# A modulation ring of four places in x's memory instead of two places of its own, for the first projection of a two-block transformer kernel

## The chip, the cores and the metric

One core of one Trainium2 chip runs the whole kernel in one launch. The metric is the device time of that core in microseconds, as the median of several executions. The engines that matter here are TensorE (PE; PEld is its weight load), VectorE (DVE), ScalarE (ACT), GpSimd (POOL) and SyncE (SP), whose queue issues most of the DMA transfers in the order in which they stand there.

## What is computed

Two transformer blocks on one sequence of 256 tokens of width 2048, in float32. The first block mixes by HGRN2 and gated delta heads, the second by four kinds of attention. Both take six modulation vectors from a small input c. Cut to what matters:

```python
def first_block(x, c, w_ada, b_ada, ..., w_in, ...):
    mod = silu(c) @ w_ada + b_ada                       # 2048 x 12288
    sh_m, sc_m, gt_m, sh_f, sc_f, gt_f = split(mod, 6)
    h = rmsnorm(x, pre_mix_norm) * (1.0 + sc_m) + sh_m
    proj = h @ w_in                                     # 2048 x 8208
    o_hg  = hgrn2_group(proj[..., :HG_COLS], ...)
    o_gdn = gdn_group(proj[..., HG_COLS:], ...)
    y = concat(o_hg, o_gdn) @ w_out
    x = x + gt_m * rmsnorm(y, post_mix_norm)
    ...
def reference(...):
    return second_block(first_block(x, ...), c_2, ada_w_2, ..., w_in_2, ...)
```

The parts of `mod` after the first two (sh_m, sc_m) are needed only after the mixing, so their columns of `w_ada` are loaded and summed in the background of other phases.

## The kernel before, in words

x is kept transposed in SBUF as `core.xT` (16 KB a partition). The first projection (`phase_in_1`, line 1594) computes h @ w_in in float32 accuracy from three products of rounded parts: each weight tile is split by ScalarE into a high part (L1983) and by VectorE into a low part (L2142, the weight less its high part), and TensorE makes high x high (L1826), high x low (L1833) and low x high (L1835). A piece of this work is a **slot**: a weight tile of 128 x 512. Four slots are a **group**, and one refill of 1 MB in two halves of 512 KB brings its weights; eight groups (32 slots) are a **turn**; there are eight turns. The parts lie in four places (`w`, KG = 4), so ScalarE may be at most four slots ahead of TensorE. Between the slots a `Pace` runs the head work of HGRN2 and the convolutions: programs that go on at slots written out by hand. In slots 34 and on, TensorE also multiplies the 16 gate columns (`gates()`, L1713), whose weights ScalarE's queue loads after slot 22 (L1991).

**SP's queue.** The weights lie in a ring of two groups, so refill g can only be issued when the subtraction in group g - 2 is done (`refill`, L104: the first half waits for that group's third slot, the second for its fourth). For turn i, refill q is thus issued at about slot 4q - 5 of the turn. Behind some refills stand loads of w_ada for the modulation (`ada.load_when_free`, L241), 512 KB each, eight a turn in turns 2 to 7. They go round a ring, and load q waits until VectorE has done the steps that used that place before:

```python
        steps = KT * self.per_turn
        queue.wait_ge(self.core.ada_steps, i * steps + (KT * self.chunks0 + AK * (q - self.slots + 1)))
```

While such a wait lasts, everything behind it in SP's queue stands. Which load stands behind which refill is written out in `AFTER_REFILL` (L1581; numbers from 8 on are loads 0 and 1 of the next turn), and `BEHIND_PAIR` (L1582) for turn 1. VectorE's 16 steps of a turn (L284, L288, two for each load) run in slots 2 + 3n/2 of the turn, that is 2, 3, 5, 6, 8, 9, ... 20, 21, 23, 24, each after the subtraction of its slot. Load 3 is thus used in slots 11 and 12, load 6 in 20 and 21, load 7 (steps 14 and 15) in 23 and 24. The ring has two places and lies in the eight tiles `GG` of `core.big`, where the last turn's output goes at the end.

In slots 28 to 59 VectorE makes 32 steps for two other chunks (`pair_ada`). Their loads are issued by POOL's queue (L238; the first four as soon as the parts of h are made, just ahead of slot 27). VectorE's queue is in order: if the first pair load is not there, the subtraction of slot 29 stands behind the step that waits for it.

**What follows.** `phase_gdn` (L2166) makes the gated delta heads; its loads of w_ada go by POOL and SP has no program in it. x is read again in the entry to the first feed-forward part. In the second block's mixer (`phase_mixer`, L2813) x is stored to device memory (`core.x_kept`, L3213), its place is used for weight parts, and it is loaded back at the end (L2886). The mixer has a modulation ring of its own with `MOD_RING` = 4 places of 256 KB (L3258, steps at L3355 and L3359, 16 steps in 48 slots).

Of the kernel before, what the change touches and what calls it, by code (L numbers as in the profile page):

```python
# [29 lines left out]
HH = 8  # L30
# [130 lines left out]
AK = 2  # L161
ASLOTS = 4
FIRST_ASLOTS = 10
IN_1_ASLOTS = 2
# [31 lines left out]
class Ada:  # L196
# [4 lines left out]
    def __init__(self, ctx, nc, core, parts, turns, slots=ASLOTS, ring=None, acc=None, folded=True, rows=None):  # L201
        self.slots, self.landed, self.folded = slots, core.ada_landed[slots], folded
# [5 lines left out]
        self.landed0, self.chunks0 = core.ada_landed_n[slots], core.ada_chunks  # L208
        core.ada_landed_n[slots] += turns * self.per_slot
# [1371 lines left out]
AFTER_REFILL = {2: (2, 3), 3: (4,), 4: (5,), 5: (6, 7), 6: (8,), 7: (9,)}  # L1581
# [9 lines left out]
ADA_SUM_SLOT, GATE_SLOT, GATE_LOAD_SLOT = 28, 34, 22  # L1591


def phase_in_1(nc, core, t, w_ada, w_in):
# [32 lines left out]
    with ExitStack() as ctx:  # L1627
        s = {n: ctx.enter_context(nc.semaphore(n)) for n in steps}
        for_heads = Ring(ctx, nc, "hgrn_bank", (4, 5, 6))
        ring = flat(GG, HH).rearrange("p (s k n) -> p s k n", s=IN_1_ASLOTS, k=AK)  # L1630
# [16 lines left out]
                  rows=ada_rows[:, 2:])  # L1647
# [28 lines left out]
        @block.sync  # L1676
        def _(sp):
            setup_sync(sp)
            for g in range(2 * QUARTERS - 2, st.groups):
                i, q = g // st.unit, g % st.unit  # L1680
                refill(sp, core, st, i, q)
                for n in (BEHIND_PAIR if i == 1 else AFTER_REFILL).get(q, ()):
                    if 2 <= i + n // st.unit < st.turns:
                        ada.load_when_free(sp, i - 2 + n // st.unit, n % st.unit)
            prefetch(sp, core, core.streams["out_1"])
# [20 lines left out]
        def _(pe):  # L1706
            def gates():
                yield from pace.until(GATE_SLOT)
                pe.wait_ge(core.gates_in_x_moved, 16)
# [136 lines left out]
        def _(act):  # L1846
# [129 lines left out]
            for slot in range(SLOTS):  # L1976
# [12 lines left out]
                if slot == GATE_LOAD_SLOT:  # L1989
                    with nc.allow_non_contiguous_dma("the 16 gate columns"):  # L1990
                        act.dma_start(core.w_gates[:], w_in[0, :, 8192:8208].rearrange("(k p) n -> p k n", p=P)  # L1991
                                      ).then_inc(core.gates_in_x_moved, 16)
                if i and slot % TILES in (0, 2):
# [172 lines left out]
def phase_gdn(nc, core, w_ada):  # L2166
# [22 lines left out]
    with ExitStack() as ctx:  # L2189
# [35 lines left out]
        made = {}  # L2225

# [582 lines left out]
MOD_CHUNK, MOD_CHUNKS, MOD_SLOT, MOD_SLOTS, MOD_RING = 16, 2, 56, 56, 4  # L2809
# [3 lines left out]
def phase_mixer(nc, core, entry, mix, t, w_ada_2):  # L2813
# [28 lines left out]
    with ExitStack() as ctx:  # L2842
# [22 lines left out]
        mod_ring = spare[:, 0:8, :].rearrange("p a b -> p (a b)").rearrange("p (s n) -> p s n", s=MOD_RING)  # L2865
# [15 lines left out]
        def _(sp):  # L2881
# [5 lines left out]
            sp.wait_ge(core.gates_in_x_moved, 48)  # L2887
# [183 lines left out]
        def _(act):  # L3071
# [120 lines left out]
            def high(c, kg):  # L3192
                g, width = st.first + 4 * c + kg, IN_2[c][1]
                for k in range(KG):
# [9 lines left out]
                    elif k % 2 == 0:  # L3204
                        if MIX_DEEP_SLOT + KG <= slot < MIX_DEEP_SLOT + 2 * KG:
                            act.wait_ge(core.gates_in_x_moved, 32)
# [340 lines left out]
def build(nc, t, out):  # L3547
    with ExitStack() as ctx:
# [33 lines left out]
        core.ada_landed = {n: [sem(f"ada_landed_{n}_{s}") for s in range(n)] for n in (IN_1_ASLOTS, ASLOTS, FIRST_ASLOTS)}  # L3582
        core.ada_landed_n = {IN_1_ASLOTS: 0, ASLOTS: 0, FIRST_ASLOTS: 0}
# [121 lines left out]
```

## Time and profile before

| what | us |
|---|---|
| median of 3 runs | 2793.84 |
| lowest and highest | 2792.79, 2795.73 |
| the execution that was profiled, timed | 2793.61 |
| its span in the profile | 2791.9 |
| first projection, slots 0 to 255 | about 47 to 548 |
| gated delta phase | 554 to about 640 |
| mixer of the second block | about 1525 to 1900 |

In a row of a timeline stand the start in us, the time in us from the first to the end of the last instruction merged into it, engine, line, operation, out<-in and the count; in square brackets the idle time of the engine before it and what ended it. "SPq" is SP's queue issuing transfers. In a row of waits stand the sum of us, how many times, and the longest. A row of a stretch has the busy us of each engine with its count of instructions, TensorE's granted clock (PEclk, share of 2.4 GHz), the mean busy share of the 16 DMA engines, and GB/s.

### The profile page before, as it was taken

The numbers are of one execution on the slowest core, as the hardware profiler recorded it, in microseconds if no ns is written. First come the engines' busy times: TensorE is split into PE (matmuls) and PEld (weight loads), VectorE is DVE, ScalarE is ACT, GpSimd is POOL, SyncE is SP. The second block draws the span as 40 slices with busy tenths as digits, with TensorE's granted clock in tenths as the row PEclk, the third lists the DMA queues.
The fourth block names the chain that finished last, engine by engine and source line by source line (L and its number), as shares of the span: only waits on it lengthen the run. The fifth ranks groups of instructions, "written<-read, shape, count | busy, mean of one in ns | idle before, by whom it ended". The sixth has DMA issues, their size and how long they took to land. (4 is left out here: it accounts for less than half of the span.)

```text
span 2791.9 us, 49277 instructions
## 1 busy us (share of the span) xinstructions
PE 2666.6 (96%) x18997; PEld 2382.1 (85%) x18997; DVE 1950.2 (70%) x2726; ACT 1393.1 (50%) x2232; POOL 305.7 (11%) x447
## 2 busy tenths in 40 slices
PE   7899999988999999999999999998999999999998
PEld 4579998887878888999998898887878888889998
DVE  2288987677777777898998566656787655555564
ACT  3355757645455555445444454555344444444454
POOL 1011413031011111121211010001011000000000
PEclk9999999999999999999999999999999999999999
DMA  9777676536488878898994765537578655655564
GB/s 364 296 261 234 227 238 195 194 114 228 158 282 275 277 270 277 309 335 307 319 336 141 207 205 159 149 114 247 191 272 293 218 181 181 193 186 186 177 195 133
DMA packets 290452, 636.57 MB, mean 228 GB/s; under 512 B 30754, under 2 KB 51686, under 8 KB 289766
## 3 DMA queue, kind: packets, MB, share of 16 engines
q1 hardware_dynamic: 239264, 486.88, 52.8%
q0 software_dynamic: 39424, 142.62, 14.7%
q10 hardware_dynamic: 11590, 4.64, 0.7%
q8 instruction: 122, 2.00, 0.3%
q14 instruction: 52, 0.43, 0.0%
HBM read 629.87 MB, written 4.19 MB: 227 GB/s over the span
## 5 line engine op out<-in xcount | busy, mean ns | idle before, releaser
L1229 DVE TENSOR_TENSOR weight_parts<-weights,weight_parts 128x1024 fp32r<-128x1024 f32 x584 | 707.2, 1221 | 267.3 <-ACT weight_parts L1149 265.9
L1149 ACT ACTIVATE weight_parts<-weights 128x1024 fp32r<-128x1024 f32 x584 | 607.4, 1057 | 572.4 <-PE accumulators L1340 225.7
L1329 PE MATMUL accumulators<-h_parts,weight_parts 128*128 128x512 f32 x2816 | 776.8, 397 | 20.7 <-DVE h_parts L1216 8.5
L1329 PEld LDWEIGHTS accumulators<-h_parts,weight_parts 128*128 128x128 f32 x2816 | 484.1, 190 | 91.7 <-DVE h_parts L872 10.1
L1340 PEld LDWEIGHTS accumulators<-h_parts,weight_parts 128*128 128x128 f32 x2944 | 451.4, 190 | 73.3 <-DVE weight_parts L1229 13.0
L1340 PE MATMUL accumulators<-h_parts,weight_parts 128*128 128x256 f32 x2944 | 472.5, 282 | 9.0 <-DVE weight_parts L1229 8.9
L1833 PE MATMUL accumulators<-in_h_parts,in_weight_parts 128*128 128x256 f32 x1024 | 263.6, 289 | 20.7 <-DVE in_weight_parts L2142 20.4
L2142 DVE TENSOR_TENSOR in_weight_parts<-weights,in_weight_parts 128x512 fp32r<-128x512 f32 x256 | 186.2, 745 | 113.6 <-ACT in_weight_parts L1983 113.0
L1835 PE MATMUL accumulators<-in_h_parts,in_weight_parts 128*128 128x256 f32 x1024 | 260.0, 286 | 0.0
L1373 PE MATMUL accumulators<-h_parts,weight_parts 128*128 128x512 f32 x864 | 236.5, 395 | 2.8 <-issue 1.8
L1983 ACT ACTIVATE in_weight_parts<-weights 128x512 fp32r<-128x512 f32 x256 | 154.9, 627 | 147.6 <-PE accumulators L1835 103.9
L1833 PEld LDWEIGHTS accumulators<-in_h_parts,in_weight_parts 128*128 128x128 f32 x1024 | 199.0, 194 | 26.4 <-DVE in_weight_parts L2142 25.8
L1393 PE MATMUL accumulators<-h_parts,weight_parts 128*128 128x256 f32 x864 | 216.8, 283 | 0.1
L1395 PE MATMUL accumulators<-h_parts,weight_parts 128*128 128x256 f32 x864 | 216.6, 283 | 0.0
L1835 PEld LDWEIGHTS accumulators<-in_h_parts,in_weight_parts 128*128 128x128 f32 x1024 | 199.1, 194 | 0.0
L1826 PE MATMUL accumulators<-in_h_parts,in_weight_parts 128*128 128x256 f32 x1024 | 179.2, 298 | 15.1 <-DVE in_h_parts L1661 9.6
L1826 PEld LDWEIGHTS accumulators<-in_h_parts,in_weight_parts 128*128 128x128 f32 x1024 | 144.2, 195 | 44.9 <-issue 23.9
L1373 PEld LDWEIGHTS accumulators<-h_parts,weight_parts 128*128 128x128 f32 x864 | 147.7, 189 | 23.3 <-issue 2.1
L1393 PEld LDWEIGHTS accumulators<-h_parts,weight_parts 128*128 128x128 f32 x864 | 165.9, 192 | 0.5 <-DVE weight_parts L1229 0.5
L1395 PEld LDWEIGHTS accumulators<-h_parts,weight_parts 128*128 128x128 f32 x864 | 165.9, 192 | 0.0
L288 DVE SCALAR_TENSOR_TENSOR ada_sums<-h_t,c_act,ada_sums 128x512 f32<-128x512 f32 x224 | 159.8, 746 | 4.6 <-DMA h_t<-in_ada_w 4.4
L238 POOL DMA_DIRECT2D h_t<-in_ada_w x112 | 80.3, 718 | 720.9 <-DVE ada_sums L288 238.7
(426 smaller groups left out, 3702.2 us busy)
## 6 DMA issues: line engine op xcount, KB each, us to landing
weights<-in_w_ff SPq DMA_DIRECT2D x256, 512.0 KB, 5.8
weights<-in_w_in SPq DMA_DIRECT2D x160, 512.0 KB, 5.3
wide<-in_w_ada SPq DMA_DIRECT2D x112, 512.0 KB, 10.0
h_t<-in_ada_w POOLq DMA_DIRECT2D x112, 512.0 KB, 6.7
weights<-in_ffn_w_gate SPq DMA_DIRECT2D x88, 512.0 KB, 4.6
weights<-in_ffn_w_up SPq DMA_DIRECT2D x88, 512.0 KB, 4.5
weights<-in_ffn_w_down SPq DMA_DIRECT2D x88, 512.0 KB, 4.2
weights<-in_w_out SPq DMA_DIRECT2D x64, 512.0 KB, 5.6
```

The source lines that it names most:

```text
L288: ins = nc.vector.scalar_tensor_tensor(out=acc, in0=w, scalar=number, in1=acc, op0=ALU.mult, op1=ALU.add)
L1149: nc.scalar.activation(w[:, held:held + take, 0, :], core.ring[:, q % RING, k:k + take, :], ACT.Copy).then_inc(core.high_ready, take)
L1229: ins = nc.vector.tensor_tensor(w[:, held:held + take, 1, :], core.ring[:, q % RING, k:k + take, :], w[:, held:held + take, 0, :].bitcast( ...
L1329: nc.tensor.matmul(both(nt), high, x[:, kt].rearrange("p a t -> p (a t)"), start=(kt == 0), stop=False, skip_group_check=True)
L1340: ins = nc.tensor.matmul(rest(nt) if two else acc(c, nt), w[:, held, 1, nt * P:(nt + 1) * P], x[:, kt, 0, :], start=False, stop=(kt == KT ...
L1373: nc.tensor.matmul(both(nt), w[:, held, 0, cols[nt]], xk.rearrange("p a t -> p (a t)"), start=first, stop=False, skip_group_check=True)
L1393: nc.tensor.matmul(accs[nt], w[:, held, 0, cols[nt]], xk[:, 1, :], start=False, stop=False, skip_group_check=True)
L1395: ins = nc.tensor.matmul(accs[nt], w[:, held, 1, cols[nt]], xk[:, 0, :], start=False, stop=(last and nt % 2 == 1), skip_group_check=True)
L1826: nc.tensor.matmul(acc(c, nt), w[:, k, 0, nt * P:(nt + 1) * P], x[:, kt, 0, :], start=(kt == 0 and nt % 2 == 0), stop=False, skip_group_ch ...
L1833: nc.tensor.matmul(acc(c, nt), w[:, k, 0, nt * P:(nt + 1) * P], x[:, kt, 1, :], start=False, stop=False, skip_group_check=True)
L1835: ins = nc.tensor.matmul(acc(c, nt), w[:, k, 1, nt * P:(nt + 1) * P], x[:, kt, 0, :], start=False, stop=(kt == KT - 1 and nt % 2 == 1), sk ...
L2142: ins = nc.vector.tensor_tensor(w[:, k, 1, :], core.ring[:, g % RING, part, :], w[:, k, 0, :].bitcast(F32), ALU.subtract)
```

## The change

The first projection's modulation ring gets four places and moves into the memory of x. To make room, x is stored to device memory by ScalarE's queue after slot 26 (2 MB) and loaded back by SP's queue at the start of the gated delta phase. SP waits for the store before the first load into the new ring (behind refill 15), and the gates' products wait for a count of 32 on the same semaphore, so for the store as well. The table of loads becomes one load behind each refill from 1 to 6 and two behind refill 7: load 7, before behind refill 5, now stands behind refill 6, and loads 2 and 3 behind refills 1 and 2. The ring gets semaphores of its own, and the mixer's ring shrinks from four places to two. The counts that later waits name go up by 32.

```diff
-IN_1_ASLOTS = 2
+IN_1_ASLOTS = 4
...
+    def __init__(self, ctx, nc, core, parts, turns, slots=ASLOTS, ring=None, acc=None, folded=True, rows=None, landed=None):
+        landed = landed or slots
+        self.slots, self.landed, self.folded = slots, core.ada_landed[landed], folded
...
-AFTER_REFILL = {2: (2, 3), 3: (4,), 4: (5,), 5: (6, 7), 6: (8,), 7: (9,)}
+AFTER_REFILL = {1: (2,), 2: (3,), 3: (4,), 4: (5,), 5: (6,), 6: (7,), 7: (8, 9)}
 BEHIND_PAIR = {7: (8, 9)}
...
+X_KEPT_SLOT = 26
...
-        ring = flat(GG, HH).rearrange("p (s k n) -> p s k n", s=IN_1_ASLOTS, k=AK)
+        ring = core.xT[:].rearrange("p a b -> p (a b)").rearrange("p (s k n) -> p s k n", s=IN_1_ASLOTS, k=AK)
...
                 refill(sp, core, st, i, q)
+                if g == 2 * st.unit - 1:
+                    sp.wait_ge(core.gates_in_x_moved, 32)
                 for n in (BEHIND_PAIR if i == 1 else AFTER_REFILL).get(q, ()):
...
             def gates():
                 yield from pace.until(GATE_SLOT)
-                pe.wait_ge(core.gates_in_x_moved, 16)
+                pe.wait_ge(core.gates_in_x_moved, 32)
...
+                if slot == X_KEPT_SLOT:
+                    act.dma_start(core.x_kept, core.xT[:].rearrange("p a b -> p (a b)")
+                                  ).then_inc(core.gates_in_x_moved, 16)
...
+        @block.sync
+        def _(sp):
+            sp.dma_start(core.xT[:].rearrange("p a b -> p (a b)"), core.x_kept).then_inc(core.gates_in_x_moved, 16)
+            sp.wait_ge(core.gates_in_x_moved, 48)
...
-MOD_CHUNK, MOD_CHUNKS, MOD_SLOT, MOD_SLOTS, MOD_RING = 16, 2, 56, 56, 4
+MOD_CHUNK, MOD_CHUNKS, MOD_SLOT, MOD_SLOTS, MOD_RING = 16, 2, 56, 56, 2
...
-        mod_ring = spare[:, 0:8, :].rearrange("p a b -> p (a b)").rearrange("p (s n) -> p s n", s=MOD_RING)
+        mod_ring = spare[:, 0:2 * MOD_RING, :].rearrange("p a b -> p (a b)").rearrange("p (s n) -> p s n", s=MOD_RING)
...
-            sp.wait_ge(core.gates_in_x_moved, 48)
+            sp.wait_ge(core.gates_in_x_moved, 80)
...
-                            act.wait_ge(core.gates_in_x_moved, 32)
+                            act.wait_ge(core.gates_in_x_moved, 64)
```

## Rows read from the trace of the kernel before

**Rows 1.** Head of the page.
```profile
span 2791.9 us, 49277 instructions
```

**Rows 2.** Busy times of stretches of the first projection.
```profile
150.00:200.00 50.00, 50.00 (x351) 40.51 (x350) 41.33 (x75) 24.18 (x33) 6.59 (x9) 1.00 0.72 251
...
318.00:378.00 60.00, 53.26 (x519) 51.23 (x518) 55.52 (x71) 42.42 (x82) 24.55 (x24) 1.00 0.65 217
...
435.00:500.00 65.00, 65.00 (x508) 58.97 (x507) 40.72 (x56) 45.84 (x90) 12.59 (x16) 1.00 0.62 198
```

**Rows 3.** Waits from 200 to 552 us: sum, times, longest.
```profile
ACT in_weight_parts L1983 <- DMA weights<-in_w_in: 27.3, 16, 4.1
...
PE accumulators L1833 <- DVE in_weight_parts L2142: 18.9, 17, 2.1
...
DVE turn_sums L288 <- DMA wide<-in_w_ada: 1.3, 2, 1.1
```

**Rows 4.** VectorE in order of time, in turns 4, 5 and 7.
```profile
352.37 2.27 DVE L2142 TENSOR_TENSOR in_weight_parts<-weights,in_weight_parts 128x512 fp32r<-128x512 f32 x2
...
358.07 0.74 DVE L288 SCALAR_TENSOR_TENSOR turn_sums<-wide,c_act,turn_sums 128x512 f32<-128x512 f32 x1
...
361.05 0.69 DVE L2142 TENSOR_TENSOR in_weight_parts<-weights,in_weight_parts 128x512 fp32r<-128x512 f32 x1 [1.33 <-ACT in_weight_parts L1983]
...
406.18 1.28 DVE L2142 TENSOR_TENSOR in_weight_parts<-weights,in_weight_parts 128x512 fp32r<-128x512 f32 x2
...
412.59 0.74 DVE L288 SCALAR_TENSOR_TENSOR turn_sums<-wide,c_act,turn_sums 128x512 f32<-128x512 f32 x1
...
530.77 1.29 DVE L2142 TENSOR_TENSOR in_weight_parts<-weights,in_weight_parts 128x512 fp32r<-128x512 f32 x2
...
535.40 0.74 DVE L288 SCALAR_TENSOR_TENSOR turn_sums<-wide,c_act,turn_sums 128x512 f32<-128x512 f32 x1
538.49 0.69 DVE L2142 TENSOR_TENSOR in_weight_parts<-weights,in_weight_parts 128x512 fp32r<-128x512 f32 x1 [2.35 <-ACT in_weight_parts L1983]
```

**Rows 5.** SP's queue in turn 3: loads 2 and 3.
```profile
265.32 7.15 SPq L238 DMA_DIRECT2D wide<-in_w_ada  x2
```

**Rows 6.** SP's queue at the end of turn 1: loads 0 and 1.
```profile
195.78 4.17 SPq L238 DMA_DIRECT2D wide<-in_w_ada  x2
```

**Rows 7.** Landing of loads at L238: at 214.6 us, at 502.3 us, all 46 after 210.
```profile
DMA to landing us min/median/max: 7.0/7.0/7.0
...
DMA to landing us min/median/max: 6.2/6.2/6.2
...
DMA to landing us min/median/max: 3.6/4.7/7.0
```

**Rows 8.** Busy times of stretches around the end of turn 0.
```profile
125.00:130.00 5.00, 3.97 (x32) 3.90 (x33) 3.38 (x5) 1.73 (x4) 3.03 (x4) 1.00 0.07 9
...
135.00:140.00 5.00, 2.94 (x13) 2.94 (x14) 0.69 (x1) 1.83 (x4) 0.00 (x0) 0.51 1.03 413
140.00:145.00 5.00, 3.54 (x16) 3.25 (x16) 3.39 (x7) 2.34 (x7) 0.72 (x1) 0.50 0.94 317
```

**Rows 9.** VectorE's first pair step and TensorE's product that waits behind it.
```profile
141.17 0.49 DVE L284 TENSOR_SCALAR turn_sums<-wide,c_act 128x512 f32<-128x512 f32 x1 [3.43 <-DMA wide<-in_w_ada]
...
142.31 0.58 PE L1833 MATMUL accumulators<-in_h_parts,in_weight_parts 128*128 128x256 f32 x1 [1.46 <-DVE in_weight_parts L2142]
```

**Rows 10.** The mixer: landing of x_kept's store, of the refill behind, of five before.
```profile
DMA to landing us min/median/max: 9.0/9.0/9.0
...
DMA to landing us min/median/max: 8.7/8.7/8.7
...
DMA to landing us min/median/max: 3.1/3.2/4.5
```

**Rows 11.** A stretch early in the gated delta phase.
```profile
560.00:565.00 5.00, 5.00 (x24) 2.96 (x23) 2.65 (x6) 3.11 (x5) 4.30 (x11) 1.00 0.45 177
```

**Rows 12.** VectorE in the mixer behind the ring's first three steps.
```profile
1619.72 1.09 DVE L3468 TENSOR_TENSOR in_weight_parts<-weights,in_weight_parts 128x896 fp32r<-128x896 f32 x1 [3.04 <-ACT in_weight_parts L3210]
```

More of the change, by code:

```diff
@@ L196 @@
 class Ada:
-    def __init__(self, ctx, nc, core, parts, turns, slots=ASLOTS, ring=None, acc=None, folded=True, rows=None):
-        self.slots, self.landed, self.folded = slots, core.ada_landed[slots], folded
+    def __init__(self, ctx, nc, core, parts, turns, slots=ASLOTS, ring=None, acc=None, folded=True, rows=None, landed=None):
+        landed = landed or slots
+        self.slots, self.landed, self.folded = slots, core.ada_landed[landed], folded
         self.nc, self.core, self.turns = nc, core, turns
@@ L207, in __init__ @@
         self.per_slot = self.per_turn * AGROUPS // slots
-        self.landed0, self.chunks0 = core.ada_landed_n[slots], core.ada_chunks
-        core.ada_landed_n[slots] += turns * self.per_slot
+        self.landed0, self.chunks0 = core.ada_landed_n[landed], core.ada_chunks
+        core.ada_landed_n[landed] += turns * self.per_slot
         core.ada_chunks += turns * self.per_turn
@@ L1646, in phase_in_1 @@
         ada = Ada(ctx, nc, core, [(w_ada, 0, 2 * NT + 2, 1)], LAST - 1, IN_1_ASLOTS, ring, pair_ada.acc,
-                  rows=ada_rows[:, 2:])
+                  rows=ada_rows[:, 2:], landed="in_1")
         taps = big[:, HG:HG + 6, :].rearrange("p (a b) t -> p a b t", a=2)
@@ L3581, in build @@
         core.scaled, core.factored = sem("input_normalized"), sem("input_factored")
-        core.ada_landed = {n: [sem(f"ada_landed_{n}_{s}") for s in range(n)] for n in (IN_1_ASLOTS, ASLOTS, FIRST_ASLOTS)}
-        core.ada_landed_n = {IN_1_ASLOTS: 0, ASLOTS: 0, FIRST_ASLOTS: 0}
+        core.ada_landed = {name: [sem(f"ada_landed_{name}_{s}") for s in range(n)] for name, n in (
+            ("in_1", IN_1_ASLOTS), (ASLOTS, ASLOTS), (FIRST_ASLOTS, FIRST_ASLOTS))}
+        core.ada_landed_n = {"in_1": 0, ASLOTS: 0, FIRST_ASLOTS: 0}
         core.ada_steps, core.ada_sums_ready, core.ada_sums_taken = (
```

## Prediction

> **What bounds the kernel now.** I read four views in this order. First the page's head: the span is 2791.9 us, and the same execution was timed at 2793.61 us [rows 1]. The sum below is made against that 2793.61; the median of the three runs is 2793.84, 0.2 us away, so the one stands for the other. Then the busy times by stretch inside the first projection, where the ring that changes is used [rows 2]. From 435 to 500 us TensorE is busy for 65.00 of 65 us. From 318 to 378 it is idle for 6.7 us while VectorE is busy for 55.5 of 60. So a turn is bound by TensorE where its extra products are many and by VectorE where the head work is, while the DMA engines are at about two thirds. Third, the waits from 200 to 552 us [rows 3]: ScalarE waits 27.3 us for refills in 16 places, which is what the change can remove. But TensorE's idle time, 18.9 us, is put down to VectorE's subtraction of the low parts, not to a load. What earlier refills can give back is therefore not 27.3 us, only the part of the 18.9 us for which VectorE itself was short of work. Fourth, VectorE in order of time [rows 4]: it stood idle for a refill's high part for 1.33 us before 361.05 and for 2.35 us before 538.49. I found no third such place ahead of a gap of TensorE, so the gain in sight is at most 3.7 us.
>
> **Part 1, SP's queue.** Today load 3 stands in SP's queue ahead of refill 3, and its wait (for VectorE's step at slot 6) ends only as that refill's place comes free. The two loads hold SP from 265.32 to 272.47, and the refill goes out behind them [rows 5]. Load 7 does the same ahead of refill 6. With four places these waits are satisfied long before, so the first halves of the two refills leave about 1 us earlier (one step of VectorE and the issue) in each of six turns. The same holds at the hand-over to turn 2, where the pair's last steps keep SP until 199.95 before refill 16 [rows 6]: that refill comes some 3 us earlier, but ScalarE then waits for TensorE's last tile of the turn anyway. I count nothing for it, and up to 1 us in the range.
>
> **Part 2, load 7.** The new list puts load 7 straight behind refill 6. Refill 6's second half waits for VectorE's subtraction in slot 19 of the turn; load 7 is used by step 14, in slot 23, after that slot's subtraction. Today load 7 leaves at slot 18, alone. What does a load take that leaves straight behind a refill? Load 2 does so today in each of six turns, and lands 6.2 to 7.0 us after its own issue (the last and the first of the six), which is 0.4 us behind the second half's [rows 7]. I take 6.6 + 0.4 = 7.0 us. Turn 4: slot 19's subtraction ends at 353.5 (the first of the two at 352.37), so the load lands at 360.5; step 14 is due at 358.07, and from there to the idle stretch before 361.05 there are 1.65 us of work, so slot 24's subtraction comes at 362.15, not 361.05: 1.1 us later. Turn 5: 406.8 + 7.0 = 413.8 against step 14 at 412.59: 1.2 us. Turn 7: 531.4 + 7.0 = 538.4, and 0.74 us of work, is 539.1 against 538.49: 0.7 us [rows 4]. All three lie just ahead of a place where TensorE waits for VectorE, so I pass them on whole. In turns 2 and 3 I reckon with half a microsecond where TensorE has slack, in turn 6 with none. Sum: 3.0 us. Note that the two idle stretches which could be won, in turns 4 and 7, are the very ones in which load 7 is late now: the refill is no longer late, the load behind it is. Bounds: 0 (the quickest of 46 loads lands in 3.6 us [rows 7]) and 5. Loads 2 to 6 have five slots or more to land, loads 8 and 9 ten: 0. SP's new wait before loads 8 and 9 of turn 1 is for a store issued four refill groups and more earlier: 0.
>
> **Part 3, x goes out.** ScalarE's queue issues a store of 2 MB after slot 26; the issue itself costs nothing, since ScalarE then idles for refill 7. But the store meets the worst place of the phase. The gate columns' load has kept the DMA engines at 9 GB/s; once it is through, all that has queued (two refills, the pair's four first loads) moves at 413 and 317 GB/s with the engines full [rows 8]. 2.10 MB more at 413 GB/s is 5.1 us. And a delay here finds no slack: VectorE waits 3.43 us for the first pair load, until 141.17; its next subtraction is what TensorE waits 1.46 us for, at 142.31 [rows 9]; from 150 to 200 us TensorE is busy for 50.00 of 50 [rows 2]. The nearest row for what such a store does to its neighbours is in the mixer: the same store takes 9.0 us, and a refill issued 2 us behind it takes 8.7 where five before it took 3.2 in the median, so it is held for 5.5 us [rows 10]. Bounds: 0 (the pair load, issued just before the store, goes wholly ahead) and 5.5. I take 4.5, near the upper end, because a part of that load is through before the store starts. Refill 8, behind the store, lands up to 5 us later too; ScalarE may run four slots ahead of TensorE, which is itself 4.5 us later by then: covered. The gates' products now wait for the store at slot 34, five slots after the stall, by when it has landed: 0, at most 1. TensorE's granted clock is 0.51 and 0.50 from 135 to 145, the lower of its two levels (1.2 GHz), after it idled [rows 8, 9]; a longer idle moves that stretch along and may lengthen it by 0 to 3 us; I take 0.
>
> **Part 4, x comes back.** 2 MB on SP's queue at the start of the delta phase, beside the loads there. From 560 to 565 us the DMA engines are at 0.45 [rows 11], SP has nothing else to do in that phase, and x is first read after it. What hides the load is that idle DMA time; without it it would cost about 5 us. I take 0, in the range 0 to 1.
>
> **Part 5, the mixer.** Its modulation ring has two places instead of four, so a load leaves only when the step before the previous one has ended. Steps are three slots apart by the code, and loads of twice the size land in 4.7 us in the median [rows 7]. Only the third load, whose steps come bunched at the start, would be late, by up to 3 us, and VectorE idles 3.04 us right behind it, before 1619.72 [rows 12]. 0, at most 1.
>
> **Sum.** 3.0 + 4.5 = 7.5 us: 2793.6 + 7.5 = 2801.1 us. The own range of this case is 2798 to 2806.
>
> **Rivals.** A measurement of this kernel can tell about 0.2% (5.6 us) from no change.
> (A, the forecast) The store and the late load 7 both cost: 2801.1. Chance 0.50, nine tenths of it past 5.6 us.
> (B) The store shares the DMA engines evenly instead of going first. The pair load then has a third of the engines where it had a half for its last 2 to 3 us, which costs 1 to 2.5 us: 1.8 + 3.0, so 2798.4. Against it speaks the refill of [rows 10], held for 5.5 of the store's 9.0 us; even sharing would have cost it about half. Chance 0.20, nearly all of it within 5.6 us.
> The Trainium skill states a rule for B ("DMA: Bandwidth & Descriptors", section "Issuing engines are not separate DMA queues"): transfers that different engines start run on the same DMA engines and interleave there. By that rule the total would be 2798.4, by the mixer's row 2801.1; rule and row differ, and I go by the row.
> (C, faster) The refills were what mattered: refills 3 and 6 leave 1 us earlier and no load is in flight beside them, so ScalarE is four slots ahead at every piece of head work, and the backlog of VectorE to which TensorE's 18.9 us are put down does not form. For it: 27.3 us of waiting for refills in 16 places [rows 3]. Against it: VectorE's 55.5 busy us of 60 where TensorE idles most [rows 2]. It decides if more than half of the 18.9 us goes and the store costs under 2: 2793.6 - 10 + 2 = 2785.6. Chance 0.18, of which 0.16 past 5.6 us.
> (D) The change does nothing that can be seen: the pair load is ahead of the store, and load 7 lands in 4 us. 2793 to 2795. Chance 0.12.
>
> **Range and chances.** 2790 to 2806.5 leaves out most of C and a small tail of A (a longer stretch at the low clock). Faster 0.16; within 5.6 us 0.36 (D, nearly all of B, the edges of A and C); slower 0.48.
>
> **What would show it.** The store: VectorE's wait for the first pair load grows from 3.4 to about 8 us, and TensorE's product that now starts at 142.3 starts near 147; if it stays where it is, part 3 is wrong. Load 7: VectorE's waits for the loads of w_ada come to over 3 us against 1.3 now [rows 3]; if they don't grow, part 2 is wrong. ScalarE's 27.3 us of waiting for refills should fall below 15 in any case but D; if TensorE's 18.9 us fall with them to under 10, C was right. The mixer and the delta phase should last as long as before within 1 us.

## The result, and the profile after

The changed kernel takes 2805.7 us (median of 19 runs) against 2792.8 us for the kernel before (19 runs beside them). The ratio is 1.0043, with a 95% interval of 1.0035 to 1.0052: 12 us slower, 10 to 14.5 by the interval. The forecast was 2801.1, slower, in a range of 2790 to 2806.5. The execution that was profiled took 2801.95 us, so the terms read from its profile add up to 8 us, not 12. One of the 19 runs took 3209.97 us and is not part of the ratio.

The head of the profile's page after; the span grew by 8.0 us [rows 1]:

```profile
span 2799.9 us, 49281 instructions
```

**The stop at the end of turn 0.** VectorE's first step for the pair, TensorE's product behind it, and two stretches (columns as in [rows 8]):

```profile
145.65 0.49 DVE L285 TENSOR_SCALAR turn_sums<-wide,c_act 128x512 f32<-128x512 f32 x1 [8.29 <-DMA wide<-in_w_ada]
```

```profile
146.79 0.58 PE L1837 MATMUL accumulators<-in_h_parts,in_weight_parts 128*128 128x256 f32 x1 [6.10 <-DVE in_weight_parts L2149]
```

```profile
140.00:145.00 5.00, 0.69 (x4) 0.49 (x3) 0.00 (x0) 0.57 (x2) 0.00 (x0) 0.84 1.00 415
145.00:150.00 5.00, 3.21 (x15) 3.21 (x16) 4.09 (x8) 2.39 (x6) 0.72 (x1) 0.50 0.86 301
```

The wait for the first pair load went from 3.43 to 8.29 us, TensorE's from 1.46 to 6.10 [rows 9]. From 140 to 145 the DMA engines are full while hardly any other engine works. TensorE starts again at the lower of its two clock levels, as before [rows 8], only five microseconds later.

**Who was issued first.** ScalarE and its queue (ACTq), POOL's queue, and the landing of the store (L1998):

```profile
123.17 1.06 ACT L1658 ACTIVATE in_h_parts<-h_t 128x1024 fp32r<-128x1024 f32 x1
123.39 0.38 ACTq L1998 DMA_DIRECT2D x_kept<-x_t  x1
124.13 2.18 ACT L1987 ACTIVATE in_weight_parts<-weights 128x512 fp32r<-128x512 f32 x4
```

```profile
124.89 3.04 POOL L239 DMA_DIRECT2D wide<-in_w_ada  x4 [110.64 <-ACT in_h_parts L1658]
```

```profile
DMA to landing us min/median/max: 22.0/22.0/22.0
```

The store leaves at 123.39, 1.5 us ahead of the four pair loads. They wait for the end of ScalarE's last high part of h (the 123.17 row, at 124.2). In ScalarE's program the store stands behind that instruction and behind the high parts of slots 24, 25 and 26, the first three of the 124.13 row, and yet it was issued before any of these three began: the issue didn't wait for the instructions ahead of it to run. I had the order the other way round. The store landed at 145.4, together with the first pair load (145.65).

**Load 7 and the other loads of w_ada.** Waits from 200 to 570 us (sum, times, longest), the landing of SP's 46 loads of w_ada, and VectorE where it waited for one: for load 7 in turn 4 (365.71), for load 6 and then load 7 in turn 5 (414.63 and 420.29), for load 7 in turn 7 (546.27):

```profile
PE accumulators L1837 <- DVE in_weight_parts L2149: 22.6, 22, 3.3
...
DVE turn_sums L289 <- DMA x_t<-in_w_ada: 8.6, 5, 3.4
ACT in_weight_parts L1987 <- DMA weights<-in_w_in: 7.9, 7, 2.6
```

```profile
DMA to landing us min/median/max: 5.2/6.7/9.2
```

```profile
365.71 1.22 DVE L289 SCALAR_TENSOR_TENSOR turn_sums<-x_t,c_act,turn_sums 128x512 f32<-128x512 f32 x1 [2.90 <-DMA x_t<-in_w_ada]
...
414.63 0.75 DVE L289 SCALAR_TENSOR_TENSOR turn_sums<-x_t,c_act,turn_sums 128x512 f32<-128x512 f32 x1 [0.98 <-DMA x_t<-in_w_ada]
...
420.29 0.75 DVE L289 SCALAR_TENSOR_TENSOR turn_sums<-x_t,c_act,turn_sums 128x512 f32<-128x512 f32 x1 [0.79 <-DMA x_t<-in_w_ada]
...
546.27 0.75 DVE L289 SCALAR_TENSOR_TENSOR turn_sums<-x_t,c_act,turn_sums 128x512 f32<-128x512 f32 x1 [3.42 <-DMA x_t<-in_w_ada]
```

Read against [rows 3]: ScalarE's waits for refills fell from 27.3 to 7.9 us, just what the ring was for. TensorE's waits for VectorE rose from 18.9 to 22.6 all the same, because VectorE now waits 8.6 us for loads of w_ada against 1.3. A load that leaves behind a refill lands in 6.7 us in the median; before, it was 4.7 [rows 7].

**Stages.** Start of a slot's first product, and the end of slot 255's four products high x high, in us, from the timelines of one profiled execution each (e1 to e10 are the experiments below; the slot's other eight products take 1.0 us more in each, so the first projection of the kernel before ends at 553, not at 548 as the table ahead of the prediction has it):

| | before | after | e1 | e2 | e3 | e9 | e10 |
|---|---|---|---|---|---|---|---|
| slot 28 | 137.1 | 136.7 | 137.1 | 136.5 | 136.5 | 137.1 | 137.2 |
| slot 32 | 147.6 | 152.4 | 147.7 | 152.1 | 145.6 | 153.0 | 153.0 |
| slot 64 | 209.2 | 214.1 | 209.3 | 213.7 | 207.3 | 214.7 | 214.6 |
| slot 255 | 552.1 | 560.5 | 559.1 | 554.1 | 548.7 | 558.1 | 564.3 |
| slot 64 to there | 342.9 | 346.4 | 349.8 | 340.4 | 341.4 | 343.4 | 349.7 |
| output projection starts | 642.9 | 651.7 | 647.4 | 643.8 | 639.3 | 649.5 | 656.4 |
| mixer's first product | 1523.7 | 1532.8 | 1531.2 | 1521.3 | 1520.6 | 1533.2 | 1540.5 |
| span | 2791.9 | 2799.9 | 2798.3 | 2788.9 | 2787.0 | 2801.4 | 2808.0 |
| runs, median | 2792.8 | 2805.7 | 2799.8 | 2798.0 | 2789.4 | 2801.0 | 2804.3 |

So after has +4.8 by slot 32 and +3.5 between slot 64 and the end of the phase; from there to the output projection +0.4; nothing more behind it.

The same stretch by turns, from the start of a turn to the start of the next (turn 7: to the start of slot 255), in us. e4 and e9 have the old ring and the old table of loads:

| turn | before | e4 | e9 | after | e10 | e1 | e2 | e3 |
|---|---|---|---|---|---|---|---|---|
| 2 | 52.5 | 52.5 | 52.5 | 53.1 | 53.3 | 53.3 | 52.5 | 52.5 |
| 3 | 56.6 | 56.6 | 56.8 | 55.7 | 55.8 | 55.7 | 55.7 | 55.7 |
| 4 | 59.4 | 60.2 | 59.8 | 61.0 | 61.0 | 60.4 | 58.8 | 59.8 |
| 5 | 57.1 | 57.2 | 57.2 | 58.6 | 59.4 | 58.8 | 58.3 | 58.3 |
| 6 | 64.8 | 64.8 | 64.8 | 64.8 | 64.8 | 64.8 | 64.8 | 64.8 |
| 7 | 51.8 | 53.6 | 51.7 | 52.6 | 54.7 | 56.1 | 49.6 | 49.6 |

After, e10 and e1 have load 7 behind refill 6; e2 and e3 have it behind refill 5.

**x back, and the mixer.** A stretch of the delta phase in which x comes back (its load is issued at 562.5), and VectorE behind the third load of the mixer's ring:

```profile
565.00:570.00 5.00, 5.00 (x29) 3.50 (x29) 2.39 (x10) 1.97 (x5) 4.55 (x10) 1.00 0.94 396
```

```profile
1623.61 0.75 DVE L3371 SCALAR_TENSOR_TENSOR wide<-wide,c_act 128x512 f32<-128x512 f32 x1
1627.47 1.09 DVE L3480 TENSOR_TENSOR in_weight_parts<-weights,in_weight_parts 128x896 fp32r<-128x896 f32 x1 [3.11 <-ACT in_weight_parts L3222]
```

TensorE is busy for 5.00 of 5 us while the DMA engines are at 0.94. In the mixer the third step (1623.61) shows no wait, and the idle time behind it is what it was (3.11 against 3.04 [rows 12]).

### The profile page after: what moved, and what is told of

It is laid out like the page before. It is cut to its first block and busy times, and to the rows that moved or that the text cites. A ratio compares the mean times of both kernels' runs of the same rounds, so it can differ in the third digit from the quotient of the medians.

```text
span 2799.9 us, 49281 instructions
## 1 busy us (share of the span) xinstructions
PE 2670.5 (95%) x18997; PEld 2385.2 (85%) x18997; DVE 1949.3 (70%) x2726; ACT 1393.2 (50%) x2232; POOL 302.8 (11%) x447
## 3 DMA queue, kind: packets, MB, share of 16 engines
q1 hardware_dynamic: 239408, 488.98, 53.1%
## 5 line engine op out<-in xcount | busy, mean ns | idle before, releaser
L1330 PE MATMUL accumulators<-h_parts,weight_parts 128*128 128x512 f32 x2816 | 778.8, 398 | 18.9 <-DVE h_parts L1217 8.5
L1374 PEld LDWEIGHTS accumulators<-h_parts,weight_parts 128*128 128x128 f32 x864 | 147.7, 189 | 24.0 <-DVE weight_parts L1230 2.1
```

The lines of the kernel that those rows point to most:

```text
L1330: nc.tensor.matmul(both(nt), high, x[:, kt].rearrange("p a t -> p (a t)"), start=(kt == 0), stop=False, skip_group_check=True)
L1374: nc.tensor.matmul(both(nt), w[:, held, 0, cols[nt]], xk.rearrange("p a t -> p (a t)"), start=first, stop=False, skip_group_check=True)
```

## The experiments

Theory 1: the store costs the time of its own bytes at the end of turn 0. Theory 2: load 7 behind refill 6 is late for its step. The rivals are told with each run.

**e1: the store later, after slot 44.** By then the pair's loads and the queued refills are through.

```diff
-X_KEPT_SLOT = 26
+X_KEPT_SLOT = 44
...
-                pe.wait_ge(core.gates_in_x_moved, 32)
+                pe.wait_ge(core.gates_in_x_moved, 16)
```

> The changed kernel with x's store after slot 44 instead of slot 26, and the gates' products waiting for their own columns alone. Theory 1 (the store costs 4.8 us because it meets the full DMA engines ahead of the first pair load): VectorE's wait for that load is back at 3.4 us, TensorE's product of slot 29 back at 142.3, slot 64 starts near 209.2 instead of 214.1, and the total falls by about 4.8 us against the changed kernel, so it stands at +3 to +7 us to the kernel before (the changed kernel at +8 in its profile, +12 in its runs). At slot 44 the DMA engines are at about 0.8, so up to 1 us of it may come back there. Rival (the cost comes from the gates' longer wait or from the ring lying in x): slot 29 stays near 147 or a new gap of 4 to 5 us stands at slot 34, the total stays.

Measured: 2799.8 us, ratio to the kernel before 1.0025 [1.0016, 1.0035], so +7.0. Slot 64 starts at 209.3 against 209.2 in the kernel before: the store's 4.8 us are gone to within 0.1. What is left is all behind slot 64, 349.8 us against 342.9, and that is 3.4 more than in the changed kernel itself. The stretches at the end of turn 7 tell why (columns as before):

```profile
540.00:545.00 5.00, 2.45 (x20) 2.25 (x20) 1.83 (x3) 1.67 (x3) 0.00 (x0) 1.00 0.53 205
545.00:550.00 5.00, 4.09 (x20) 3.80 (x19) 4.68 (x8) 0.63 (x1) 0.00 (x0) 0.51 0.03 9
550.00:555.00 5.00, 5.00 (x37) 5.00 (x36) 1.88 (x3) 1.90 (x3) 0.00 (x0) 0.81 0.64 207
```

TensorE stood for half of 540 to 545 (load 7 again), and from 545 to 550 its granted clock is 0.51, the lower level: 20 products in 4.09 busy us. From slot 240 to the end of the phase e1 takes 30.3 us where the changed kernel's profile has 26.8: 1.0 of these 3.5 us is longer idle time (gaps of 2.55 and 0.91 us against 0.70 and 1.76), and the other 2.5 are the clock, which in the changed kernel's profile stayed at 1.00 at that place:

```profile
545.00:550.00 5.00, 3.68 (x29) 3.27 (x27) 3.62 (x6) 2.41 (x4) 0.00 (x0) 1.00 0.51 206
550.00:555.00 5.00, 3.87 (x32) 3.87 (x33) 4.09 (x7) 1.26 (x2) 0.00 (x0) 1.00 0.39 107
```

**e2: load 7 back behind refill 5.** The store stays after slot 26.

```diff
-AFTER_REFILL = {1: (2,), 2: (3,), 3: (4,), 4: (5,), 5: (6,), 6: (7,), 7: (8, 9)}
+AFTER_REFILL = {1: (2,), 2: (3,), 3: (4,), 4: (5,), 5: (6, 7), 6: (8,), 7: (9,)}
```

> The changed kernel with loads 6 and 7 behind refill 5, 8 behind refill 6 and 9 behind refill 7, as before, all else as changed. Theory 2 (load 7 behind refill 6 lands late): VectorE's waits for the w_ada loads fall from 8.6 us to under 1.5, the last slot ends 3 to 4 us earlier relative to slot 64 than in the changed kernel (346.4 us from slot 64 to the end of slot 255 there, 342.9 before), so 342 to 343.5; total 3 to 4 us below the changed kernel. Rival (the 3.6 us between slot 64 and the end are not load 7 but VectorE's backlog, which the shift re-deals): the waits fall but the stretch stays at 345 to 347 us.

Measured: 2798.0 us, ratio 1.0021 [1.0011, 1.0031], +5.9. The waits from 200 to 556 us:

```profile
PE accumulators L1837 <- DVE in_weight_parts L2149: 18.6, 18, 3.0
...
ACT in_weight_parts L1987 <- DMA weights<-in_w_in: 12.6, 9, 2.2
...
DVE turn_sums L289 <- DMA x_t<-in_w_ada: 1.5, 1, 1.5
```

VectorE's 8.6 us of waits for w_ada are 1.5 now, and slot 64 to the end takes 340.4 us, 6.0 less than after and 2.5 less than before. The store's share is untouched (slot 64 at 213.7). The execution that was profiled took 2790.95 us, 7 below e2's median, so its span, 3.0 us below that of the kernel before, doesn't stand for the runs. Of turn 5 nothing came back: 58.3 us against 57.1 before, and the one wait that is left is VectorE's for load 6 of that turn (landed 7.2 us after its issue, before 4.8). e3 has the same 58.3.

**e3: both edits.**

> Both edits together: x's store after slot 44 and load 7 behind refill 5. If both theories hold and add up, 8.4 us come off the first projection and the total is within 2 us of the kernel before, perhaps 1 to 3 us below it, because the refills 3 and 6 still leave 1 us earlier and ScalarE's wait for refills stays under 15 us. Rival (four places are worth something once the two costs are gone): 5 us or more below the kernel before. If the total stays 4 us or more above the kernel before, a third cost outside the first projection (x's way back, the mixer's ring) is real.

Measured: 2789.4 us, ratio 0.9985 [0.9975, 0.9996]: 4.2 us faster than the kernel before, and 16 faster than the changed one. This version beats both. Its waits, and the stretch in which the kernel before ran at the lower clock:

```profile
ACT in_weight_parts L1987 <- DMA weights<-in_w_in: 11.2, 8, 2.4
...
DVE turn_sums L289 <- DMA x_t<-in_w_ada: 2.0, 2, 1.6
```

```profile
140.00:145.00 5.00, 3.45 (x28) 3.31 (x28) 3.99 (x7) 2.97 (x7) 0.72 (x1) 0.96 0.88 298
```

From 140 to 145 it has 28 products at a clock of 0.96 where the kernel before has 16 at 0.50 [rows 8]. Slots 28 to 32 take 9.1 us against 10.5. I don't know that this comes with every execution; nothing in the edit is about these slots, and e4, with the old code there, has 9.1 too. Set against these quicker slots the store costs more: 6.4 us between the profiles of e3 and e2 (slot 64 at 207.3 and 213.7), where it costs 4.8 between e1 and the changed kernel.

**e4: the kernel before with two places in the mixer's ring, that part alone.**

```diff
-MOD_CHUNK, MOD_CHUNKS, MOD_SLOT, MOD_SLOTS, MOD_RING = 16, 2, 56, 56, 4
+MOD_CHUNK, MOD_CHUNKS, MOD_SLOT, MOD_SLOTS, MOD_RING = 16, 2, 56, 56, 2
```

> The kernel before with only the mixer's modulation ring cut from four places to two. By part 5 of the prediction: same as before within 1 us, no new gap of TensorE in the mixer, the third step late by up to 3 us in front of an idle stretch of VectorE. Rival (the difference between the changed kernel's +8 us in its profile and +12 us in its runs comes from the mixer): 3 to 4 us slower.

Measured: 2792.4 us, ratio 0.9998 [0.9986, 1.0010]. The smaller ring costs nothing that the runs can see (the interval is -3.9 to +2.8 us). Its profile also serves as a measure of chance: its slot 32 starts at 145.2, 2.4 us sooner than in the kernel before, from the same code up to there. A difference of 2 us at that place in one profile proves nothing.

**e5: e2 with the store after slot 28**, so that it is issued behind the pair loads.

```diff
-X_KEPT_SLOT = 26
+X_KEPT_SLOT = 28
```

> The kernel of the second run (load 7 early) with x's store after slot 28 instead of 26, so that it is issued at about 136 us, when the pair's four first loads and refills 7 and 8 already stand in their queues; in the changed kernel it was issued at 123.4, 1.5 us ahead of the first of them. Theory 1a (what counts is who is issued first): the first pair load lands near 141 again, VectorE waits 3.4 to 4.5 us for it instead of 8.3, slot 32 starts at 147 to 149 instead of 152, and refills 8 and 9 land a few us later without a gap. Rival 1b (the store goes first or takes the larger share once it is there, whenever it was issued): the pair load lands at 144 to 146 and slot 32 starts at 150 to 152.

One execution, 2793.7 us beside 2792.3. VectorE's two waits, and the landing of the store, issued at 135.0:

```profile
139.69 0.49 DVE L285 TENSOR_SCALAR turn_sums<-wide,c_act 128x512 f32<-128x512 f32 x1 [3.32 <-DMA wide<-in_w_ada]
...
147.04 0.75 DVE L289 SCALAR_TENSOR_TENSOR turn_sums<-wide,c_act,turn_sums 128x512 f32<-128x512 f32 x1 [5.27 <-DMA wide<-in_w_ada]
```

```profile
DMA to landing us min/median/max: 12.2/12.2/12.2
```

The time of one execution can't tell these cases apart; the waits can. The first pair load is back where it was (3.32 against 3.43 [rows 9]), as theory 1a has it, and the second pays instead: 5.27 us. Slot 32 starts at 150.3, which is the rival's range. Slot 28 to slot 64 takes 77.4 us, as in the changed kernel (77.4) and against 72.1 before. To be issued behind the loads doesn't save the loads; it only changes which of them is late.

**e6: e2 with two stores after slot 26**, the second to memory that nothing reads.

```diff
+                    act.dma_start(x_kept_again, core.xT[:].rearrange("p a b -> p (a b)")
+                                  ).then_inc(core.gates_in_x_moved, 16)
```

> The kernel of the second run with x stored twice after slot 26, the second time to a buffer that nothing reads; the gates' products and SP wait for both. Theory 1 (the store's cost is the DMA engines' time for its bytes, 5.1 us for 2 MB, with no slack behind it): a further 4.5 to 5.5 us, VectorE's wait for the first pair load at about 13 us, slot 32 at about 157. Rival (a fixed cost of waiting or ordering, not of bytes): slot 32 stays at 152 to 153.

One execution, 2804.9 us.

```profile
144.83 0.49 DVE L285 TENSOR_SCALAR turn_sums<-wide,c_act 128x512 f32<-128x512 f32 x1 [8.27 <-DMA wide<-in_w_ada]
...
152.18 0.75 DVE L289 SCALAR_TENSOR_TENSOR turn_sums<-wide,c_act,turn_sums 128x512 f32<-128x512 f32 x1 [5.26 <-DMA wide<-in_w_ada]
```

Slot 64 starts at 218.8, 5.1 us behind e2's 213.7, and 5.7 behind if both are counted from the start of slot 28: the second 2.10 MB cost 5.1 to 5.7 us, and 2.10 MB at 413 GB/s [rows 8] is 5.1. The wait for the first pair load didn't grow to 13 us as expected (8.27); the second store landed at 152.0, with the second pair load, the first at 144.6, with the first.

**e7: e1 with load 7 moved once more, behind refill 7.** More of theory 2's cause.

```diff
-AFTER_REFILL = {1: (2,), 2: (3,), 3: (4,), 4: (5,), 5: (6,), 6: (7,), 7: (8, 9)}
+AFTER_REFILL = {1: (2,), 2: (3,), 3: (4,), 4: (5,), 5: (6,), 7: (7, 8, 9)}
```

> The kernel of the first run (late store) with load 7 behind refill 7 instead of refill 6, four slots later still, in each of six turns. Theory 2 (a load lands 7 us behind the refill that it follows, and VectorE's queue stands until then): the load leaves with slot 23's subtraction and is wanted by the very next step, so VectorE waits about 6.5 to 7 us in each turn, 40 us in all, and TensorE, at most four slots ahead of it in parts, passes on a third to two thirds of it: the stretch from slot 64 to the end grows from 346 to 350 us to 365 to 380. Rival (TensorE's time in the turns is set by other work and the wait is absorbed): it stays under 355.

One execution, 2828.3 us. Waits from 200 to 600 us:

```profile
DVE turn_sums L289 <- DMA x_t<-in_w_ada: 43.7, 8, 7.6
PE accumulators L1837 <- DVE in_weight_parts L2149: 41.9, 23, 5.6
```

Slot 64 to the end takes 379.1 us, at the upper end of what theory 2 expected. VectorE's waits for w_ada grew by 34 us from e1's 9.8 and the stretch by 29. Not all of the 29 is waiting: TensorE is idle for 39.8 us of the stretch against 21.4 in e1, 18.4 more, and busy for 340.3 us against 329.3 with the same products. The 11.0 us of longer busy time come with a granted clock of 0.50 in five of the stretches of 5 us (320 to 325 and 385 to 390 among them) where e1 has one such (545 to 550, 0.51).

**e8: e3 with the gate columns loaded by POOL's queue at the very start**, where nothing multiplies yet.

```diff
+                pool.dma_start(core.w_gates[:], w_in[0, :, 8192:8208].rearrange("(k p) n -> p k n", p=P)
+                               ).then_inc(core.gate_columns_in, 16)
...
-                if slot == GATE_LOAD_SLOT:
-                        act.dma_start(core.w_gates[:], w_in[0, :, 8192:8208].rearrange("(k p) n -> p k n", p=P)
-                                      ).then_inc(core.gates_in_x_moved, 16)
```

The waits that count on these semaphores follow, and two small loads at the start of the kernel share the semaphore of the loads beside them, so one wait there covers two loads more; no run tells what that alone costs.

> The kernel of the third run (store after slot 44, load 7 early) with the 16 gate columns loaded by GpSimd's queue at the very start of the kernel instead of by ScalarE's after slot 22, on a semaphore of their own. Theory 3 (the gate columns' load of 2048 pieces of 64 bytes holds up every transfer behind it from 117 to 132 us, and the stop at 132 to 142 is its doing): no stretch of idle DMA engines at 117 to 132, the gaps of TensorE before slots 28 and 29 (4.9 and 1.5 us) and VectorE's wait of 3.4 us vanish, and 6 to 9 us come off by slot 32, if the same hold-up at the start is hidden behind the loads' way to the first slot. Rival (the hold-up only moves: it delays the first loads of x and of the modulation by as much): slot 0 starts 5 to 15 us later and the total is the same or up to 8 us slower.

Measured: 2794.2 us, ratio 1.0011 [0.9998, 1.0023], 5 us slower than e3 by the medians, 7 by the two ratios. The first 20 us, and the landing of that load:

```profile
0.00:20.00 20.00, 0.31 (x1) 0.18 (x1) 0.00 (x0) 0.00 (x0) 12.33 (x39) 1.00 0.94 81
```

```profile
DMA to landing us min/median/max: 21.1/21.1/21.1
```

The hold-up moved, it didn't go: the kernel before moves 324 GB/s in its first 20 us, this one 81. Slot 0 starts at 61.1 us against 47.5 in e3; 7 of these 13.7 us are won back by slot 32, where the old stop is no more. The rival to the idea (the load holds everything wherever it stands) was right.

**e9: the kernel before with the store alone** after slot 26, nothing else of the change.

```diff
+                if slot == 26:
+                    act.dma_start(core.x_kept, core.xT[:].rearrange("p a b -> p (a b)")
+                                  ).then_inc(core.gates_in_x_moved, 16)
```

> The kernel before with one thing added: x is stored after slot 26 (the gates' products wait for it; the ring, the table of loads and the mixer are the old ones, and nothing is loaded back). Theory 1 (the store costs its own DMA time, about 5 us, once, and nothing else): slot 64 starts at 213.5 to 214.5 us against 209.2 in the kernel before, slot 64 to the end of the phase lasts as before (342.9, within 2 us), and the runs give 2797.5 to 2798.5 us, a ratio of 1.0016 to 1.0020. Rival (the store costs more in the timed runs than the one profile shows, which would explain why the changed kernel's runs are 12 us above the kernel before and its profile only 8): slot 64 again near 214, but the runs give 2801 us or more, a ratio over 1.0028. A third outcome, below 2795, would mean that the store costs only together with the new order of the loads.

```profile
146.05 0.49 DVE L284 TENSOR_SCALAR turn_sums<-wide,c_act 128x512 f32<-128x512 f32 x1 [8.31 <-DMA wide<-in_w_ada]
```

```profile
147.19 0.58 PE L1833 MATMUL accumulators<-in_h_parts,in_weight_parts 128*128 128x256 f32 x1 [5.98 <-DVE in_weight_parts L2145]
```

The profile gives the change's own stop (8.31 and 5.98 against 8.29 and 6.10), with slot 64 at 214.7 (+5.5) and 343.4 us from there to the end of the phase (+0.5). So the store is a cause by itself, without the new ring and the new table. The runs say 2801.0, ratio 1.0029 [1.0017, 1.0041], +8.1: above what I expected and at the rival's bound. The interval (4.7 to 11.4) holds 5.5 too. The profile's span is 9.5 us longer, and 2.9 of it lie between the output projection and the mixer, where the two programs are the same: that stretch lasts 880.8 us in the kernel before, 883.7 here, and between 877.5 (e2) and 884.1 (e10) in the profiles of the table.

**e10: the changed kernel again**, beside e9.

> The changed kernel itself, beside e9_store_alone and the kernel before on one chip, to tell how far its runs lie above it. If the terms that the profiles show are all there is (store 4.8, load 7 3.5): ratio 1.0025 to 1.0035, 2800 to 2803 us. If the timed runs hold something that the profile does not: again 1.0040 or more, 2804 us and over. The difference to e9_store_alone should be load 7's share, 3 to 4 us by the profile, 6 to 8 by the earlier runs.

Measured: 2804.3 us, ratio 1.0047 [1.0034, 1.0060]. The profiled execution took 2810.0 us, where the first one of this kernel took 2801.95. Turn 7, VectorE at step 14 and the stretches behind it:

```profile
548.58 0.75 DVE L289 SCALAR_TENSOR_TENSOR turn_sums<-x_t,c_act,turn_sums 128x512 f32<-128x512 f32 x1 [3.84 <-DMA x_t<-in_w_ada]
```

```profile
550.00:555.00 5.00, 3.24 (x21) 3.04 (x22) 4.90 (x8) 0.63 (x1) 0.00 (x0) 0.90 0.01 6
555.00:560.00 5.00, 5.00 (x35) 5.00 (x34) 1.85 (x4) 1.89 (x3) 0.00 (x0) 0.76 0.68 210
```

Slot 64 to the end: 349.7 us, where the first profile of this kernel had 346.4. Of the 3.3 us more, 1.1 came before slot 240 (TensorE's gap behind turn 5 is 4.10 us against 3.31), 0.7 is longer idle time in turn 7, and the rest, 1.5, is the clock, which is below 1.00 for the ten microseconds of the two rows. The same program thus shows 3.5 and 6.8 us behind slot 64 in two executions. The fall isn't load 7's alone, though: e4's profile, the old table of loads, has one at the same place:

```profile
540.00:545.00 5.00, 3.48 (x20) 3.48 (x21) 3.93 (x7) 0.75 (x2) 0.00 (x0) 0.75 0.30 82
545.00:550.00 5.00, 5.00 (x52) 4.80 (x52) 1.64 (x4) 1.26 (x2) 0.00 (x0) 0.91 0.69 233
```

and its slot 64 to the end takes 345.6 us where the kernel before had 342.9. The gap ahead of this fall is 1.76 us (before 541.52). The kernel before has the same 1.76 us at the same place (before 542.70) and no fall behind it, but it has falls in turn 3 (clock 0.66 from 295 to 300, behind a gap of 2.06 us) and in turn 5 (0.68 from 420 to 425, behind 1.83).

## Why the prediction was right, and where it was not

**Direction and case: right.** Case A (both the store and load 7 cost) is what happened, and undoing each part took its share away. In the profiled execution the sum was 7.5 against 8.0 measured. Against the runs it was 4.5 us short, and the runs of the parts say the same of each: e1, which has load 7's lateness without the early store, is 7.0 us above the kernel before (4.5 to 9.8) where 3.0 was forecast; e2, which has the early store without the late load 7, is 5.9 above (3.1 to 8.7), and e9 8.1 (4.7 to 11.4), where 4.5 was. So the time came out inside the range with both prices too low in the runs, load 7's most of all; that the first profile agrees with the sum so closely is in part luck, as e10 shows. Nor do the shares add up exactly: the runs lose 5.0 us of the 12 without the early store and 6.1 without the late load 7, but 16.2 without both. Each of these ratios has an interval of 2 to 3 us either way, so the missing 5 us may be noise; the runs don't settle it.

**Part 3, the store: 4.5 forecast, 4.8 in the profile after and 5.5 in e9.** By the profiles the size was right; two steps on the way were not. The first is "because a part of that load is through before the store starts": the store left first, 123.39 against 124.89. The second is the bound of 0 ("the pair load, issued just before the store, goes wholly ahead"). e5 brought that order about, and the first load was indeed spared, but the store's time was then paid at the second one. The DMA engines are full there and TensorE has no slack behind, so 2.10 MB cost about their time at 413 GB/s at each of the two places tried (e5, one execution, and e6). The prediction's own 5.1 us was the better value, and the lower bound should have been close to it.

**Case B, even sharing.** It priced the store at 1.8 by looking at the first pair load only. The Trainium skill ("DMA: Bandwidth & Descriptors", section "Issuing engines are not separate DMA queues") says that transfers started by different engines interleave. The traces agree: the changed kernel's store and first pair load land within 0.3 us of each other (145.4 and 145.65), e5's store (135.0 to 147.2) and second pair load (147.0) too. What fell is my price for it: with the store issued first, the first pair load alone was 4.9 us later, and where it wasn't late (e5) the second was.

**Part 2, load 7: 3.0 forecast; 3.5 in the profile after, 6.9 and 6.8 in e1 and e10, 7.0 in the runs of e1.** The mechanism was right (8.6 us of waits, 2.90 in turn 4 and 3.42 in turn 7 where the landing estimate gave 2.4 and 3.0). By turns the first profile has +0.6, -0.9, +1.6, +1.5, 0 and +0.8 in turns 2 to 7, where the forecast was nothing net in turns 2 and 3, then 1.1, 1.2, 0 and 0.7. In part they agree for another reason. In turn 5 the forecast put all on load 7 and nothing on load 6 ("Loads 2 to 6 have five slots or more to land ...: 0"); VectorE waited 0.98 us for load 6 and 0.79 for load 7, and with load 7 early (e2, e3) turn 5 still takes 1.2 us more than before. In turns 2 and 3 a loss of 0.6 and a gain of 0.9 cancel. The term was mis-sized by half a microsecond in the one execution, and by more in others: the waits themselves vary (8.6 to 10.4 us in sum), and a fall of the clock in turn 7 adds 1.5 to 2.5 us. I had written of the low-clock stretch at the end of turn 0 that it "may lengthen", and had no such term for turn 7, though the trace before has such falls in turns 3 and 5. The fall came in e1, e7 and e10, where load 7 is late, not in the first profile after, where it is late as well, and once (e4) where it isn't. Whether late load 7 makes it likelier, and so accounts for part of the 4 us between the profile and the runs, is not shown: only one execution of each run has a profile. That difference stays open; the untouched middle of the kernel alone differs by 6.6 us from profile to profile. The mean granted clock, which is on record for every timed execution, says only this much: within each of e1 to e4, e8, e9 and the changed kernel, the longer executions tend to have the lower clock (correlations of -0.57 to -0.72; e10, with five executions, -0.37).

**Part 1, SP's queue: counted at nothing, up to 1 us.** The gain exists, and load 7 hid it. In turn 5 the first halves of refills 3 and 6 leave 8.1 and 28.0 us into the turn (e2) against 9.1 and 29.0 before, the 1 us that was forecast. With load 7 back behind refill 5, slot 64 to the end takes 340.4 to 341.4 us in the five profiles that have it so (e2, e3, e5, e6, e8) against 342.9 to 345.6 in the three with the old ring (before, e9, e4), so 1.5 to 2.5 us against the kernel before, within the 3.7 that the prediction held to be in sight. It sits in turn 3 (0.9) and turn 7 (2.1 or more), less the 1.2 that load 6 costs in turn 5. Turn 7 was one of the two places named; in turn 4, the other, e2 and e3 lie on either side of the kernel before. The runs of e3 (4.2 us faster, 1.1 to 7.0) agree in sign.

**Case C.** ScalarE's waits for refills fell by 19.4 us, further than C needed, and TensorE's 18.9 us did not fall (22.6 after, 18.6 in e2). TensorE there waits for VectorE, which, but for the gain under part 1, was short of nothing that a refill brings. The argument against C (VectorE busy for 55.5 of 60 us) held.

**Parts 4 and 5: 0 forecast.** x back: no cost that can be told from chance. From slot 255 to the output projection the kernel before takes 90.8 us, the changed one 91.2, and the profiles of the table lie between 88.3 (e1) and 92.1 (e10), e9 without x's way back at 91.4. The mixer: no cost that can be seen (e4).

## What to carry to other kernels

A transfer that nobody waits for isn't free for that. Here, before a place where the DMA engines are full and the next engine waits for a load, it cost about its bytes at their full rate, issued ahead of the loads or behind them, and eighteen slots later it cost nothing. When a ring is enlarged, let no load go out later than it did, and look at each load's landing again, not only at the one that was moved: a load that no longer waits in the queue leaves right behind a refill and lands later for it. Here the same ring with load 7 left in its place and the store put off turned 12 us of loss into 4 of gain. And when an idle time of TensorE is priced, look at what its granted clock did behind idle times of that length in the same trace, and give the range a term for it.

## What the runs showed of the hardware beyond what I had expected

- A load of 16 gate columns (128 KB in pieces of 64 bytes) holds up the transfers of the other queues, from either of the two queues that issued it here. After slot 22, from ScalarE's queue, it takes 18.0 us to land, the DMA engines run at 9 GB/s behind it [rows 8], and half a refill that SP issues at 119.4 takes 16.9 us, a pair load that POOL issues at 125.3 takes 15.8. At the start, from POOL's queue, it took 21.1 us to land, with 81 GB/s over the first 20 us against 324 in the kernel before; the stretch of 9 GB/s is then gone (e8: 388 GB/s from 120 to 125).
- ScalarE's queue issued the store 0.22 us after the start of the high part of h, 0.84 us before that activation's end, and 0.74 us before the start of the first of three more activations that all stand ahead of it in the program. An issue in ScalarE's program is ordered only by the waits ahead of it, as far as this trace shows.
- TensorE's granted clock fell to its lower level in turn 7 behind two gaps that sum to 3.2 us (e10) and 3.5 us (e1), and not behind 2.5 us (the changed kernel's first profile). The fall cost 1.5 and 2.5 us. That it also came in e4, behind the same 1.76 us behind which it didn't come in the kernel before and in e9 (1.75), says that the length of the gap alone doesn't decide it.
